# Splitting an output projection's matmuls into two column tiles of TensorE, 64 tokens each

## What is computed

```python
D_MODEL = 1024
MIX_WIDTH = ATTN_WIDTH + REC_WIDTH          # 512 + 512

def merge_groups(oa, orec, gr, subln_w, gnorm_w, w_out, lam_init, dtype):
    B, L = oa.shape[:2]
    a = (rmsnorm(oa, subln_w) * (1.0 - lam_init)).reshape(B, L, ATTN_WIDTH).astype(dtype)
    r = (rmsnorm(orec, gnorm_w) * jax.nn.silu(gr.astype(F32))).reshape(B, L, REC_WIDTH).astype(dtype)
    return jnp.concatenate([a, r], axis=-1) @ w_out
...
        yp = yp + merge_groups(oa, orec, gr, subln_w[l], gnorm_w[l], w_out[l], lam_init, yp.dtype)
        yp = yp + hier_moe(rmsnorm(yp, norm2_w[l]), w_group[l], w_router[l], w_e_gate[l], w_e_up[l], w_e_down[l])
```

## Time and profile before

| | us |
|---|---|
| median of 3 runs | 3133.22 |
| lowest and highest run | 3130.86, 3135.81 |
| the profiled execution: its span | 3130.3 |
| of it, TensorE busy (PE) | 2847.6 |
| `mix_and_route` on TensorE, the loop and what lies around it | 1683 to 1985 in the span |

### The profile page before, as it was taken

One profiled execution on the slowest core, in us unless ns is written; L12 is line 12 of the kernel. 1 busy time (PEld: TensorE's weight loads), 2 busy tenths in 40 slices (PEclk: granted clock), 3 DMA queues, 4 the chain that ended last, 5 costly groups with the idle time before them and its releaser, 6 DMA issues. The chain is left out here.

```text
span 3130.3 us, 41253 instructions
## 1 busy us (share of the span) xinstructions
PE 2847.6 (91%) x12609; PEld 1768.4 (56%) x12610; DVE 1540.2 (49%) x3077; ACT 1025.9 (33%) x2269; POOL 430.3 (14%) x684
## 2 busy tenths in 40 slices
PE   8999999999999688989877999599999999999960
PEld 6777777777777546556555555344444444444430
DVE  2555556555555677877743555422323233232327
ACT  2333333333342255656634555101011111101108
POOL 2111111111111111212210010101110101111000
PEclk9999999999999899999988999699999999999985
DMA  6000100000010240000033222287776557675658
GB/s 233 34 24 24 40 30 23 35 32 27 23 39 25 81 153 9 10 10 8 10 100 110 92 84 86 89 317 271 260 261 234 200 216 269 229 284 191 233 189 307
DMA packets 180197, 382.80 MB, mean 122 GB/s; under 512 B 13571, under 2 KB 51203, under 8 KB 177937
## 3 DMA queue, kind: packets, MB, share of 16 engines
q1 hardware_dynamic: 165808, 333.76, 29.6%
q0 software_dynamic: 14304, 48.08, 4.0%
HBM read 310.73 MB, written 71.08 MB: 122 GB/s over the span
## 5 line engine op out<-in xcount | busy, mean ns | idle before, releaser
L656 PE MATMUL z_psum<-w_in_sb,hT 128*128 128x512 f32 x1088 | 480.5, 592 | 0.0
L650 PE MATMUL z_psum<-hT,w_in_sb 128*128 128x128 f32 x3264 | 374.4, 276 | 0.8 <-ACT hT L326 0.8
L650 PEld LDWEIGHTS z_psum<-hT,w_in_sb 128*128 128x128 f32 x3264 | 370.2, 193 | 1.7 <-ACT hT L326 1.2
L1016 PE MATMUL score_psum<-att_k,q_by_map 128*128 (+3 forms) x640 | 280.2, 565 | 64.9 <-ACT probs L877 29.4
L1970 PE MATMUL gate_psum<-w_gate_sb,block_rows_T 128*128 x720 | 321.2, 599 | 5.6 <-SPq L1802 3.7
L656 PEld LDWEIGHTS z_psum<-w_in_sb,hT 128*128 128x128 f32 x1088 | 200.5, 190 | 221.0 <-issue 221.0
L1994 PE MATMUL down_psum<-w_down_sb,hidden_T 128*128 x720 | 323.7, 592 | 0.9 <-ACT hidden_T L1876 0.9
L1974 PE MATMUL up_psum<-w_up_sb,block_rows_T 128*128 x720 | 316.3, 592 | 0.0
L877 ACT ACTIVATE probs<-score_psum,neg_max 128x512 f32<-128x512 f32 (+3 forms) x320 | 196.4, 621 | 149.5 <-DVE neg_max L945 148.6
L1679 PE MATMUL y_psum<-w_out_sb,mix_T 128*128 128x512 f32 x544 | 243.6, 601 | 0.9 <-DVE mix_T L1536 0.9
L1974 PEld LDWEIGHTS up_psum<-w_up_sb,block_rows_T 128*128 128x128 f32 x720 | 136.8, 190 | 172.2 <-issue 172.2
(11 more groups left out here) (311 smaller groups left out, 3653.7 us busy)
## 6 DMA issues: line engine op xcount, KB each, us to landing
w_gate_sb<-in_w_e_gate SPq DMA_DIRECT2D x32, 2048.0 KB
w_up_sb<-in_w_e_up SPq DMA_DIRECT2D x32, 2048.0 KB, 15.2
w_down_sb<-in_w_e_down SPq DMA_DIRECT2D x32, 2048.0 KB, 18.2
expert_rows<-scratch_moe SPq DMA_DIRECT2D x17, 1024.0 KB, 8.2
w_in_sb<-in_w_in SPq DMA_DIRECT2D x7, 2048.0 KB, 19.6
scratch_z<-z_ring SPq DMA_DIRECT2D x34, 256.0 KB, 2.0
scratch_h<-h SPq DMA_DIRECT2D x17, 512.0 KB, 2.6
x_tile<-in_x_prompt SPq DMA_DIRECT2D x16, 512.0 KB
```

Source lines behind the costliest of these rows:

```text
L650: mm = pe.matmul(out[:, hd * P:(hd + 1) * P], w[:, c, col:col + P], hT[:, u, c, :], start=(c == 0), stop=(c == DC - 1))
L656: mm = pe.matmul(out[:, :], hT[:, u, c, :], w[:, c, g * HW:(g + 1) * HW], start=(c == 0), stop=(c == DC - 1))
L1016: mm = pe.matmul(sps[(BASE[i] + s) % 2][:, c, 0:kw * P], qz[:, i % 2, c, :], k[:, k0:k0 + kw, bass.ds(h * P, P)], start=True, stop=True)
```

## The change

Each matmul of a half of the projection is replaced by two. The first loads the 64 columns of `mT` that hold tokens 0 to 63 and writes partitions 0 to 63 of the PSUM bank; the second does the same for tokens 64 to 127 and partitions 64 to 127. Both stream the same 512 columns of `wo`. The two halves of the tokens so lie in two column tiles of the array, 128 rows by 64 columns each. The semaphore is incremented by the last of the 16 matmuls.

```diff
                 wait(pe, y_ok, 2 * t - 1 + half)
                 for c in range(DC):
-                    mm = pe.matmul(yps[:, half, :], mT[:, u, c, :], wo[:, c, half * HW:(half + 1) * HW],
-                                   start=(c == 0), stop=(c == DC - 1))
+                    for lo in (0, 64):
+                        mm = pe.matmul(yps[lo:lo + 64, half, :], mT[:, u, c, lo:lo + 64], wo[:, c, half * HW:(half + 1) * HW],
+                                       start=(c == 0), stop=(c == DC - 1))
                 mm.then_inc(y_ps, 1)
```

## The result

The changed kernel takes 3143.7 us (median of 5 runs) against 3132.4 us (median of 5 runs of the kernel before, taken with it): the ratio is 1.0035, with an interval of 1.0022 to 1.0047, that is 11.3 us more, between 6.9 and 14.7. It is slower, as forecast, by 11.3 us and not by the 25.7 us of the sum.

The account below looks back on a forecast made before the run. TensorE was taken to bound the output projection's stage; 14.6 us for lone records and 11.1 us at the borders made 25.7 us, added to 3130.3 and 2.9 for 3158.9 us. The range was 3140 to 3385 us.

Parts of the forecast that it names:

- the sum: Total added time forecast for the output projection: 14.6 us plus 11.1 us, 25.7 us more.
- the serial rival: Projection's column tiles run one after the other: 233.4 us for 544 more records, 3366.6 to 3377.7 us; chance 0.28.
- lone records: In each projection block the first and last narrow records run alone: 17 steps instead of 16, 14.6 us over 34 blocks.
- borders: At 68 changes between full and narrow width the array runs empty, losing 0.163 us of overlap each: 11.1 us.
- The case taken: Projection's column tiles overlap, records starting in program order: 3158.9 us, own range 3147.8 to 3171.8 us; chance 0.40.
- Doubled loads: In projection blocks, twice the weight loads are covered by going ahead under running matmuls: nothing added.
- not slower: Tile 1's first record starts beside tile 0's first, out of program order: 16 steps, 3130.1 to 3133.2 us; chance 0.09.
- Late loads: Tile 1's load waits until tile 0's second record starts, staggering pairs: 57.7 us (28.8 to 146.9) more, 3217 us; chance 0.19.

## Why the prediction was wrong

- What bounds the stage was right: TensorE is busy 269.00 of 269 us, the time moved there, the clock stayed at 1.00, and TensorE got no new wait.
- That the tiles run beside each other was right, and with it the largest part of the range fell away: the serial rival did not come, since 1088 records took the time of 544.
- The step that failed is the **lone records**, 14.6 us, "each record starting in program order". They cost nothing: a block stayed at 16 steps. TensorE takes a record of the other tile ahead of up to three waiting ones, as the runs with eight and with four in a row showed at two distances, and in the changed kernel one waits. Lone steps do appear, but only where more than that waits in between.
- The **borders**, taken at 11.1 us with 0.163 us each, were the right term by the right mechanism: loads are not taken ahead across a change of width. They were sized too high: 7.9 us in the stage, 0.12 us each. The overlap is not lost whole: at the end of a block the next load begins some 0.07 us before the last matmul's record ends, and the entry into half 1, behind the short matmuls of the ranks, costs 0.10 us. With this term alone the sum would have been 3144.3 us at the 11.1 us taken, and 3141.1 at 7.9; both lie inside the measured interval, 3139.3 to 3147.1 us.
- That 3143.7 us lies within the stated range is luck. The case taken, with its lone records, began at 3147.8 us; the range reached down to 3140, a stretch for which no case of the forecast stood, and the borders alone fell into it.
- Doubled loads cost nothing, as taken: they ran in pairs, and PEld's busy time on the line even fell from 101.6 to 75.9 us.
- The rival "not slower" had the mechanism of the starts right, and its own bound, lone records and borders together under 6.3 us, was missed by the borders alone. I gave it a low chance because every record of before stood in program order; but all matmuls of before used the whole array, so those rows could not show otherwise.
- Late loads were not seen: both loads of a pair lie within the 0.14 us of a row. The 0.08 us from a matmul to the next load, used there, were read at the first pair of a block and hold for it alone: further on, the load at 1848.31 starts with the matmul of that step.

The Trainium skill, TensorE: Matmul & The Clock Gate, Part 3, has matmuls start and end strictly in program order; the failed step agreed with it. Between column tiles this does not hold, and the measurement decides: in the run with eight in a row tile 1's first record starts at 1859.08, ahead of three records of tile 0 that stand before it in the program. Its TensorEngine Tiling, section Tiling Modes, Key Properties, says that a change of mode drains TensorE while a change of tile doesn't; the loads at 1853.44 and 1856.45 agree but for the last 0.07 us, each 0.53 us after the start of a last matmul of 592 ns.

## What to carry to other kernels

Split into column tiles where the load of the array takes longer than the streaming: loads of the tiles run side by side, and in these runs it paid even though the full width is in use. Look then for what the longer time had covered, such as the turn of a loop. Where streaming is the longer part it gained nothing, and each change between full and narrow width cost 0.1 to 0.2 us; so keep narrow matmuls together in one stretch. Alternate the tiles matmul by matmul: with eight in a row on one tile most of the overlap is gone.

## What the runs showed of the hardware

- Column tiles on float32 stream fully beside each other: 544, 1088 and 2176 records at widths 128, 64 and 32 kept TensorE busy for 243.6, 242.7 and 242.1 us.
- TensorE starts matmuls of different column tiles out of program order, past three waiting records in the two orders tried (eight and four matmuls of a tile in a row). At the end the rest of the last group runs alone: 12 of 16 records and 4 of 8.
- A load with its short matmul took 0.107 us a step at 128 columns, about 0.06 at 64 in two tiles and 0.033 at 32 in four.
- Across a change of width no load is taken ahead: it starts 0.52 to 0.53 us after the last matmul of 512 columns, in either direction.
- A wait that the view puts down to VectorE was the turn of the loop on TensorE's sequencer: covered under full-width logits of 1.70 us, it cost some 0.47 us a turn behind logits of 0.72 us.
